# Taking the unread products out of TensorE's tails, norm chains and openings in a two-layer hybrid block

## The reference, cut to what matters

```python
def modulate(h, g_pre, shift, scale):
    return rmsnorm(h, g_pre) * (1 + scale) + shift

def gated_residual(h, y, g_post, gate, weight):
    return h + weight * gate * rmsnorm(y, g_post)

def swiglu_half(h, m, k, g_pre, g_post, wg, wu, wd):
    u = modulate(h, g_pre, m[3 * k], m[3 * k + 1])
    y = (jax.nn.silu(u @ wg) * (u @ wu)) @ wd
    return gated_residual(h, y, g_post, m[3 * k + 2], MACARON_WEIGHT)

for i in range(DEPTH):
    x, ctx = swiglu_half(x, ..., 0, ...), swiglu_half(ctx, ..., 0, ...)
    ...                                     # mixer on both; in the last layer ctx gives only its final state
    x = gated_residual(x, yx @ w_out[i], norm_post[i, 1], mx[5], 1.0)
    x = swiglu_half(x, mx, 2, norm_pre[i, 2], norm_post[i, 2], ffn_w_gate[i, 1], ffn_w_up[i, 1], ffn_w_down[i, 1])
```

## Time and profile before

| | |
|---|---|
| time, median of 3 runs | 2392.99 us (2392.0 to 2395.12) |
| the profiled execution's own time | 2389.37 us |
| its span, first to last instruction | 2387.3 us |
| outside the span | 2.07 us |
| TensorE matmul busy | 2238.6 us, 94% |
| VectorE busy | 1241.7 us, 52% |
| ScalarE busy | 984.9 us, 41% |
| mean granted TensorE clock | 0.969 of full |

### The profile page before, as it was taken

The page is one execution under the profiler, slowest core; times in us unless marked ns, Lnnn a source line. Parts: engine busy times, 40 slices in busy tenths (PEclk is TensorE's granted clock), DMA queues, the critical chain, the costliest instruction groups (busy, mean ns, idle before and its releaser), DMA issues. The chain is left out here.

```text
span 2387.3 us, 28755 instructions
## 1 busy us (share of the span) xinstructions
PE 2238.6 (94%) x11753; PEld 1902.1 (80%) x11753; DVE 1241.7 (52%) x1759; ACT 984.9 (41%) x1477; POOL 224.0 (9%) x139
## 2 busy tenths in 40 slices
PE   5999999998988989999999999999999988889998
PEld 5788888876676768788888778888888776779998
DVE  4544453347769743544444445333324578855554
ACT  5444443244465343434443343222323444454443
POOL 0000000023322300100000000000001332300000
PEclk8999999999999989899999998999998999989999
DMA  6455454312332213255454441323332233334553
GB/s 219 142 171 164 159 167 159 97 56 71 90 124 87 73 53 101 76 172 163 159 169 162 150 137 56 103 90 105 119 97 69 71 107 97 107 117 131 187 179 122
DMA packets 282544, 291.05 MB, mean 122 GB/s; under 512 B 8286, under 2 KB 275502, under 8 KB 282414
## 3 DMA queue, kind: packets, MB, share of 16 engines
q1 hardware_dynamic: 281619, 287.04, 37.4%
q10 hardware_dynamic: 795, 2.18, 0.3%
HBM read 288.02 MB, written 1.18 MB: 121 GB/s over the span
## 5 line engine op out<-in xcount | busy, mean ns | idle before, releaser
L85 ACT ACTIVATE split<-raw 128x1024 fp32r<-128x1024 f32 (+1 forms) x368 | 382.8, 1040 | 938.2 <-PE bank L133 927.6
L93 DVE TENSOR_TENSOR split<-raw,split 128x1024 fp32r<-128x1024 f32 (+1 forms) x304 | 364.8, 1200 | 715.3 <-ACT split L85 715.3
L131 PE MATMUL bank<-uh,split 128*128 128x512 f32 (+1 forms) x1344 | 488.6, 364 | 1.1 <-DVE split L93 1.1
L133 PE MATMUL bank<-uh,split 128*128 128x512 f32 (+1 forms) x1344 | 488.3, 363 | 0.0
L132 PE MATMUL bank<-ul,split 128*128 128x512 f32 (+1 forms) x1344 | 488.3, 363 | 0.0
L133 PEld LDWEIGHTS bank<-uh,split 128*128 128x128 f32 x1344 | 253.9, 189 | 40.2
L131 PEld LDWEIGHTS bank<-uh,split 128*128 128x128 f32 x1344 | 254.1, 189 | 38.6 <-issue 1.5
L132 PEld LDWEIGHTS bank<-ul,split 128*128 128x128 f32 x1344 | 254.1, 189 | 36.5
L131 PE MATMUL bank<-hh,split 128*128 128x512 f32 (+1 forms) x704 | 256.6, 364 | 0.9 <-DVE split L93 0.9
L131 PE MATMUL bank<-mix_uh,split 128*128 128x512 f32 (+1 forms) x608 | 231.9, 381 | 27.2 <-POOL split L100 16.4
L133 PE MATMUL bank<-hh,split 128*128 128x512 f32 (+1 forms) x704 | 255.7, 363 | 0.0
(11 more groups left out here) (225 smaller groups left out, 2974.8 us busy)
## 6 DMA issues: line engine op xcount, KB each, us to landing
raw_mod<-in_w_mod SPq DMA_DIRECT2D x64, 1024.0 KB, 4.8
raw<-in_ffn_w_gate SPq DMA_DIRECT2D x44, 1024.0 KB, 5.1
raw<-in_ffn_w_up SPq DMA_DIRECT2D x44, 1024.0 KB, 5.1
raw<-in_w_in SPq DMA_DIRECT2D x40, 1024.0 KB, 5.1
raw<-in_ffn_w_down SPq DMA_DIRECT2D x32, 1024.0 KB, 4.9
raw<-in_w_out SPq DMA_DIRECT2D x16, 1024.0 KB, 4.9
raw<-in_ffn_w_down SPq DMA_DIRECT2D x16, 768.0 KB, 4.3
decay<-cum_rows SPq DMA_DIRECT2D x48, 256.0 KB, 3.4
```

The source lines that it names most:

```text
L85: ins = K.nc.scalar.activation(K.wh[:, half, 0:kn, :], K.raw[:, slot, 0:kn, half * P:half * P + P], ACT.Copy)
L93: ins = K.nc.vector.tensor_tensor(K.wl[:, half, 0:kn, :], K.raw[:, slot, 0:kn, half * P:half * P + P], r32(K.wh[:, half, 0:kn, :]), ALU.su ...
L131: K.nc.tensor.matmul(bank[:, 0:tn], K.wh[:, half, k, :], h, start=first and k == 0, stop=False)
L133: ins = K.nc.tensor.matmul(bank[:, 0:tn], K.wl[:, half, k, :], h, start=False, stop=last and k == kn - 1)
```

## The change

Every call of `warm_pe` and the function itself are taken out. All waits, and all instructions of the other four engines, stay as they are and in the same order.

```diff
@@ product_first_pair @@
     behind = 3
-    warm_pe(K, 8)
     pe.wait_ge(K.lo_done.sem, K.lo_done.at(2))
@@ residual_rms_pe @@
-    warm_pe(K, 6)
     for n, j in enumerate(SQUARE_ORDER):
         pe.wait_ge(K.square_ready.sem, K.square_ready.at(8 * norms_before + n + 1))
         sums_pe(K, pe, y[:, j, :], tok, n == 0, n == 7)
-    warm_pe(K, 2)
     rstd_pe(K, pe, tok, nth)
-
-
-def warm_pe(K, n):
-
-    for _ in range(n):
-        K.nc.tensor.matmul(K.bank[4][:, 0:2 * P], K.ident[:, :], K.tri[:, :, :].rearrange("p d n -> p (d n)"), start=True, stop=True)
@@ OutProduct.pe @@
-        warm_pe(K, 3)
         pe.wait_ge(K.sq_added.sem, K.sq_added.at(7))
         sums_pe(K, pe, K.sq[:, 0, :], self.tok, True, True)
-        warm_pe(K, 2)
         rstd_pe(K, pe, self.tok, self.norms)
```

## The result

The changed kernel takes 2406.09 us (median, 2402.46 to 2406.96) against 2392.99 (2391.1 to 2396.91): ratio 1.005, 95% interval 1.0035 to 1.0064. The forecast was 2404.0 us, with a range of 2397 to 2410. A second set of runs, on another occasion, gave 2407.26 against 2393.43 us, ratio 1.0052 (1.0036 to 1.0067). The profiled execution took 2406.96 us; its span is 2404.9 us.

The account below looks back on a forecast made before the run. TensorE's own list was taken as the bound in most of the kernel. Terms 15.4 - 3.2 - 2.9 + 1.1 + 0.6 = +11.0 us, on the median of 2392.99, gave 2404.0 us, 0.46% slower; range 2397 to 2410 us.

Parts of the forecast that it names:

- The clock falls before the sums: In the five tails that a norm follows, clock at half before the second chain's sums and throughout them.
- A: Second chain's sums in five tails: 64 records, 32 in the latent tail, at half clock, 0.213 us each; +15.4 us.
- B: Last four unread records of the second chain delay L275 in the four full tails; removing them gains 3.2 us.
- C: Unread matmuls in the tails' first chains partly delay real work; removing them gains 2.9 us.
- D: First chain's L275 runs at half clock in one tail in three, 0.8 us each; +1.1 us, bounds 0 and +4.
- E: Openings start at half clock: 0.3 us for each of four full ones, -0.6 for the last; +0.6, bounds -1 and +7.
- Rival 2: Openings stay cold for long, delaying the first pair of products: 8 us in place of 1.2, 2411 us; 13% chance.
- Rival 1: Second chain's sums in the tails don't get slower, records stay at 0.107 us; 2386.3 us; 4% chance.
- Rival 3: In some tails the clock outlasts the first norm chain and part of the sums run at full clock; 2396 us; 8%.
- The 57 us for all the unread matmuls: Whole kernel: the 236 records of unread matmuls, at a spacing of 0.24 us, fill 57 us of TensorE.

Follow-up runs that it names:

- e3: Kernel before with only the six unread matmuls ahead of the second chain's sums taken out of each tail; 2401.51 against 2392.09 us, ratio 1.0041.
- e5: Changed kernel with the six unread matmuls ahead of the second chain's sums put back; 2390.44 us against 2393.83 for the kernel before, ratio 0.998.
- e8: Changed kernel with every second tile's sums of the second chain left out; 2379.05 us against 2393.43 for the kernel before, ratio 0.9938.
- e2: Kernel before with only the last two unread matmuls of the second chain taken out; 2392.76 against 2392.09 us, ratio 0.9999.
- second trace: The changed kernel run once more, unaltered, for a second trace of it; 2407.26 us.
- e6: Changed kernel with the second chain's sums turned round (ones stationary, 512 squares moving); 2396.84 us against 2393.83 for the kernel before, ratio 1.0015.
- e9: Kernel before with wide sums in full tails only, keeping only the 3 and the 6 of the unread matmuls; 2381.26 us, ratio 0.994.

## Why the prediction was right, point by point

- **The clock falls before the sums, in all five tails.** Shown: 0.50 in every window over them. e3 puts it on the six, and e5, which has only these, has the full clock at the start of the sums in all five tails.
- **A, sums at half clock, +15.4.** Measured by the rows: 3.07 + 4.09 + 2.74 + 2.42 + 3.36 = 15.7 us. The price of 0.213 us a record holds in e8 as well.
- **B and C, the part that is a true cost, -3.2 and -2.9.** In the changed trace the block starts 3.12 us after the root, as worked out. With A at 15.7, D and the last tail at 1.4, and the tails at +11.2 in all, B and C together gave the 5.9 that remain, of the 6.1 forecast. B can be read by itself: from 3.74 and three times 4.03 us to 3.12 is 3.4 us. e2 adds what was not in the forecast: taken out alone, the last two give nothing that can be measured.
- **D, the first L275 at half clock, one in three, +1.1.** It was one in five: 2.07 us at 1830.07, 1.16 in the other three full tails. With small change in the others and the last tail +1.4. (One in three at 0.8 over the five tails that its bound of +4 counts would have been 1.3, not 1.1.) In the second trace it was two in five. So that the term came out near is in part luck: how often the clock has fallen by then changes from one execution to the next, at 0.9 us each.
- **E, the openings, +0.6.** The four full ones cost 0.0 and not 0.3 each; the last cost 0.2 where -0.6 was taken, since its products ran at half clock for the first 4.5 us. Sum +0.2. The other opening with 256 columns, of layer 1's mixer, the sum left out without a word; it measured 16.1 us before and after, so nothing hangs on it. That the last opening costs so little holds for this trace only: over the twelve it took 9.8 to 12.0 us. Rival 2, 8 us in its place, is refuted by the 17.9 us in twelve traces.
- **Rival 1, the sums keep their pace at half clock.** Refuted: 62 records in 13.00 us, and e8. These records take 0.213 us each at half clock; at full clock they follow each other at 0.112 in the trace of the kernel before, a little more than the 0.107 that the prediction took. The rule that the Trainium skill gives for a weight load (TensorE: Matmul & The Clock Gate, section LDWEIGHTS), the number of columns divided by 1.2, with no word on the throttle, doesn't foretell this. The load records themselves lengthen with it, from 192 to 333 ns each; whether the load or something beside it sets the pace, no run here separates.
- **Rival 3, only part of the early fall.** Not in the changed kernel, where all sums were cold; in e3 it is seen in small.
- **The sum.** Forecast +11.0, measured +13.1 by the medians and 13.8 in the second set. The tails and openings account for 11.4, so the sum holds by its terms, E's two parts excepted, which were both off by less than 1.5 us and against each other; the rest lies in the bodies, of which the forecast had nothing, and its cause stays open. The 57 us for all the unread matmuls, which no term uses, were too high: their records follow each other at 0.216 us at full clock, which gives 51.

## What to carry to other kernels

Matmuls whose result nobody reads have to be judged place by place: by what waits behind them, and by what clock the next long piece on TensorE's path runs at. Here 30 of 118 earned some 16 us and the others cost some 3. Better still was to give the waiting work another shape: the same sums with the ones stationary and 512 columns moving need a quarter of the records, had the clock back within them (e6), and with a few unread matmuls ahead took 0.6% off the kernel before (e9).

## What was not expected of the hardware

- Unread matmuls cost most where they run cold: eight of them took 6.34 us in e2's last opening, mostly at half clock, against 3.69 at full, and held real products that were ready.
- The full openings don't care. In the changed kernel TensorE starts at half clock (nine records in 4.40 us), with gaps between the input tiles, and the clock is back by 518.6, early enough for the pair to end with the last tile. Warm or cold, the pair ended 17.9 us after the block's start in every one of twelve traces.
- The time of one kernel spread more than its tails can explain: the kernel before ran between 2384.5 and 2398.9 us in 29 runs. The granted clock inside the first mixer differed between traces (0.96 to 0.98) with nothing changed there, and its length by up to 8 us; what makes the clock differ is not shown.
